# The seven products of a fast matrix multiplication in another order, in the two MLPs of a Trainium2 kernel

## The reference, cut to what matters

```python
for layer in range(2):
    h = rmsnorm(x, mix_norm_g[layer])
    if layer == 0:
        x = x + diff_attention(h, ...)
    else:
        x = x + recurrent_block(h, rec_w_x, rec_w_y, ...)    # h @ w_x and h @ w_y come first
    x = x + sqrelu_mlp(rmsnorm(x, mlp_norm_g[layer]), mlp_w1[layer], mlp_w2[layer])

def sqrelu_mlp(h, w1, w2):
    return jnp.square(jax.nn.relu(h @ w1)) @ w2
```

## Time and profile before

| | |
|---|---|
| median of 3 runs | 3581.73 us (3578.41 to 3583.86) |
| the profiled execution, its own time | 3583.34 us |
| its span, first to last instruction | 3581.2 us |
| PE busy (matmul) | 3399.5 us, 95% |
| DVE busy | 2466.7 us, 69% |
| ACT busy, POOL busy | 1558.7 us (44%), 757.0 us (21%) |
| first MLP, from the first product on PE | 651.3 to 1274.2 us |
| w_x to w_o of the recurrent layer | 1274.2 to about 1600 us |
| second MLP and its sums | about 1600 to 2246 us |

### The profile page before, as it was taken

One profiled execution on the slowest core, in us unless ns is written; L12 is line 12 of the kernel. 1 busy time (PEld: TensorE's weight loads), 2 busy tenths in 40 slices (PEclk: granted clock), 3 DMA queues, 4 the chain that ended last, 5 costly groups with the idle time before them and its releaser, 6 DMA issues. The chain is left out here.

```text
span 3581.2 us, 43257 instructions
## 1 busy us (share of the span) xinstructions
PE 3399.5 (95%) x17006; PEld 2668.2 (75%) x17006; DVE 2466.7 (69%) x2845; ACT 1558.7 (44%) x2241; POOL 757.0 (21%) x439
## 2 busy tenths in 40 slices
PE   7999999999999989999999998899989989998898
PEld 6777777878778778787878787887646778764567
DVE  4666765898888989649887989476546442374666
ACT  2355453545454436425454454116345320443551
POOL 2455551000000037420000000232211222230214
PEclk9999999999999999999999999899999999999999
DMA  4234341221111121211111210231042121202413
GB/s 168 90 127 150 112 165 70 70 67 47 48 48 47 59 89 47 96 64 47 47 48 60 68 62 1 88 124 51 21 135 60 65 106 47 74 33 65 126 69 112
DMA packets 100595, 275.27 MB, mean 77 GB/s; under 512 B 9872, under 2 KB 11824, under 8 KB 100400
## 3 DMA queue, kind: packets, MB, share of 16 engines
q1 hardware_dynamic: 77104, 206.52, 17.5%
q10 hardware_dynamic: 16384, 40.90, 3.5%
q0 software_dynamic: 6912, 25.17, 2.1%
HBM read 220.39 MB, written 47.97 MB: 75 GB/s over the span
## 5 line engine op out<-in xcount | busy, mean ns | idle before, releaser
L933 PE MATMUL tk_aux<-tk_t,tk_s_hi 128*128 128x512 f32 x2048 | 512.9, 391 | 13.8 <-ACT tk_aux L1061 7.3
L1038 ACT CAST tk_s_hi<-tk_w 128x1024 fp32r<-128x1024 f32 x224 | 235.5, 1052 | 521.0 <-PE tk_aux L933 292.5
L933 PEld LDWEIGHTS tk_aux<-tk_t,tk_s_hi 128*128 128x128 f32 x2048 | 381.3, 188 | 106.6 <-issue 19.4
L933 PE MATMUL tk_acc<-tk_t,tk_s_hi 128*128 128x512 f32 x1536 | 380.2, 390 | 0.0
L1259 DVE TENSOR_TENSOR held_lo<-tk_w,tk_s_hi 128x1024 fp32r<-128x1024 f32 x224 | 273.7, 1222 | 107.4 <-ACT tk_s_hi L1038 107.2
L933 PEld LDWEIGHTS tk_acc<-tk_t,tk_s_hi 128*128 128x128 f32 x1536 | 288.3, 188 | 60.7 <-issue 1.0
L933 PE MATMUL tk_aux<-tk_t,held_lo 128*128 128x512 f32 x1024 | 274.0, 389 | 0.0
L933 PEld LDWEIGHTS tk_aux<-tk_t,held_lo 128*128 128x128 f32 x1024 | 192.2, 188 | 40.5
L175 POOL TENSOR_TENSOR pj_w_lo<-pj_w_raw,pj_w_hi 128x1024 fp32r<-128x1024 f32 x24 | 61.8, 2578 | 702.0 <-ACT pj_w_hi L150 700.4
L933 PE MATMUL tk_acc<-tk_t,held_lo 128*128 128x512 f32 x768 | 205.3, 389 | 0.0
L841 POOL CAST held_hi<-held_raw 128x1024 fp32r<-128x1024 f32 (+1 forms) x30 | 41.5, 1384 | 710.2 <-DVE tk_t L1275 596.9
(11 more groups left out here) (474 smaller groups left out, 8196.2 us busy)
## 6 DMA issues: line engine op xcount, KB each, us to landing
tk_w<-in_w_trunk SPq DMA_DIRECT2D x128, 512.0 KB, 4.1
da_w_mod<-in_ada_w POOLq DMA_DIRECT2D x48, 512.0 KB, 4.0
pj_w_raw<-in_w_in SPq DMA_DIRECT2D x44, 512.0 KB, 3.3
held_raw<-in_w_trunk SPq DMA_DIRECT2D x26, 512.0 KB, 3.3
held_raw<-in_w_qkv SPq DMA_DIRECT2D x24, 512.0 KB, 4.2
ma_w_raw<-in_w_out SPq DMA_DIRECT2D x24, 512.0 KB, 3.3
x_dram<-xT ACTq DMA_DIRECT2D x16, 512.0 KB, 4.4
xT<-x_dram SPq DMA_DIRECT2D x16, 512.0 KB, 7.0
```

The source lines that it names most:

```text
L933: last = pe.matmul(bank, w[:, d % 2, at:at + P], tr[:, f % 2, y, k, :], start=(j in (M1, M4, M5) and k == 0 and part == 0), stop=(k == 3 a ...
L1038: act.copy(tiles(s_hi[:, d % 2, :]), left(d)).then_inc(sems["s_hi"], 1)
```

## The change

1. The order becomes M1, M2, M4, M5, M6, M7, M3. The loads, sums, takes, ReLUs and squares are re-timed to it: t3 is made two steps earlier (steps 8 and 9 instead of 10 and 11); at an even phase's end whole tiles 4 to 7 go through the ReLU first (step 13) and the half tiles 0 to 3 in the next phase's steps 0 and 1; t1, t2 and t4 of an odd phase follow in steps 1 to 3.
2. ACT takes M1 (and M4 to M6 of even phases) before the cast of the next right operand instead of behind it. In phases 0 and 8 the root, which belongs to that take, comes forward with it.
3. At both MLPs' ends the tiles come in the order 4, 5, 6, 7, 0, 1, 2, 3 (`TILES`), and part of the squares is added earlier.
4. The recurrent layer's sum (`total`) stands in the second w_x panel, ahead of its sixth tile. The third panel goes to `aux[:, 1]` and does not wait for a bank of `pn.acc`; DVE reads it there.

POOL's and SP's lists of instructions are the same, save for which block is loaded when and which unit is waited for.

```diff
-    M1, M2, M4, M5, M6, M3, M7 = range(7)
+    M1, M2, M4, M5, M6, M7, M3 = range(7)
...
                     def first_of_branch(k):
-                        if k == DK - 1:
+                        pe.wait_ge(sems["x_lo"], (k + 4) % DK + 1)
+
+                    def second_of_branch(k):
+                        if k == TILES[5]:
                             total(1, 0)
-                        pe.wait_ge(sems["x_lo"], k + 1)
...
                     pe.wait_ge(sems["read_dve"], wg.d_at[7, M7, 1])
-                    linear(R_X, first_of_branch, 1)
-                    pe.wait_ge(sems["read_dve"], wg.d_at[7, M7, 3])
-                    linear(R_X + 1, None, 3)
+                    pn.product(pe, 0, R_X // 2, *A, first_of_branch, TILES)
+                    pe.wait_ge(sems["read_dve"], wg.d_at[7, M3, 3])
+                    pn.product(pe, 1, R_X // 2, *A, second_of_branch, TILES)
+                    pn.product(pe, 0, R_X // 2 + 1, *A, bank=aux[:, 1, :], spare=True)
+                    linear(R_X + 3, None, 1)
+                    evacuated(pe, R_X + 2)
...
                                 if not (ph % 8 == 0 and d == 0 or ph % 8 == 7 and d == 13):
                                     s_high(at + 1)
-                                if ph % 2 and d < 2:
-                                    for p in (2 * d, 2 * d + 1):
-                                        square_tile(ph - 1, p)
-                                if f + 1 < 56 * m + 56:
-                                    t_high(f + 1, d % 2)
+                                if ph % 2 and d == 2:
+                                    for p in (2, 3):
+                                        square_block(ph - 1, 1, p)
...
                                     for p in (2 * q, 2 * q + 1):
                                         take(ph, jj, p)
+                                if f + 1 < 56 * m + 56:
+                                    t_high(f + 1, d % 2)
...
-                        for kind, n in (((low, 0), (low, 1)), ((low, 2), (low, 3)), ((low, 4), (low, 5)),
-                                        ((low, 6), (low, 7)) + tuple((partial(add_hidden_square, 1), n) for n in range(DK)))[step]:
+                        square = partial(add_hidden_square, 1)
+                        for kind, n in (((low, 4), (low, 5)), ((low, 6), (low, 7), (square, 4), (square, 5)),
+                                        ((low, 0), (low, 1), (square, 6)), ((low, 2), (low, 3), (square, 7), (square, 0),
+                                                                            (square, 1), (square, 2), (square, 3)))[step]:
```

More of the change, by code:

```diff
@@ L197, in credit, with product @@
             pe.sem_inc(self.sems[f"panel_done{u}"], 1)
-    def product(self, pe, u, turn, h_hi, h_lo, before_chunk=None, order=None, behind=None):
+    def product(self, pe, u, turn, h_hi, h_lo, before_chunk=None, order=None, behind=None, bank=None, spare=False):
         pe.wait_ge(self.sems[f"w_split{u}"], turn + 2)
-        pe.wait_ge(self.sems[f"psum_free{u}"], turn + 1)
+        if not spare:
+            pe.wait_ge(self.sems[f"psum_free{u}"], turn + 1)
         order = order or ([c.k for c in self.prep.chunks] if self.prep else list(range(self.kc)))
+        bank = self.acc[:, u, :] if bank is None else bank
         for k in order:
@@ L208, in product @@
                 for s in range(2):
-                    last = pe.matmul(self.acc[:, u, s * HALF:(s + 1) * HALF], w[:, u, k, :],
+                    last = pe.matmul(bank[:, s * HALF:(s + 1) * HALF], w[:, u, k, :],
                                      h[:, k, s * HALF:(s + 1) * HALF],
@@ L1194, in last @@
                     def last(step):
-                        for n in ((0, 1), (2, 3), range(4, DK))[step]:
+                        for n in ((4, 5), (6, 7), range(4))[step]:
                             final(1, n)
@@ L1386, in up @@
                                 take(*due[1])
+                            if d == 13:
+                                for p in (2, 3):
+                                    relu_tile(ph, p)
                     def down(ph, finish_step):
```

91 lines of the change are left out of this document (51 added, 40 removed).

## The result

The changed kernel takes **3596.98 us**, the median of 5 runs (3592.8 to 3602.85). The kernel before, measured beside it, has 3581.73. The ratio is 1.0043, with a 95% interval of 1.0031 to 1.0055: slower by about 15 us. The forecast was 3582.8 us in a range of 3573 to 3593, with "no change" as its likeliest case. The measured time lies outside that range: the forecast's sum was +1.05 us, and the difference is +15.2.

The account below looks back on a forecast made before the run. PE, busy 95% of the span, was taken to bound the kernel. Terms +1.15 + 0.4 + 1.0 - 1.5 = +1.05 us on the median of 3581.73 gave 3582.8 us, range 3573 to 3593.

Parts of the forecast that it names:

- no change: Whole kernel: time differs by less than a measurement can tell, about 0.2% or 7.2 us; chance 0.68.
- Part B: Eight borders from even to odd phase: loss stays, as one wait of about 2.1 us in M4; +0.4 us.
- Rival 3: Nine new waits, in M4 and panel 0, each followed by half clock: +15.3 us, 3598.1 us; 17%.
- The sign named for the forecast as a whole: Inside the MLPs: a PEclk below 1.0 in the profile after would make the whole forecast wrong.
- Rival 1: At the eight borders M4's operand comes in time and the loss goes: 21.2 us, 3561.2 us; 15%.
- Part A: Start of each MLP: DVE's reciprocals come later; +0.75 us for the second, +0.4 for the first, +1.15 us together.
- Part C: Handover to the recurrent layer: DVE and POOL collide, PE waits in panel 0, root comes later; +1.0 us.
- Part D: End of the second MLP: fewer takes behind the last split, so the last sums come earlier; -1.5 us.

Follow-up runs that it names:

- x1: Changed kernel with eight dummy matmuls on PE ahead of M4's first unit in each of the eight odd phases; 3587.66 us, ratio 1.0011.
- x2: Changed kernel with ACT's second-half squares all in step 1 and DVE's sums moved ahead of splits in odd phases; 3562.82 us, ratio 0.9944.
- x4: Changed kernel with ACT again casting M4's operand ahead of the root and M1's last two copies at each MLP's start; 3594.48 us, ratio 1.0036.
- x5: Changed kernel with DVE's squares at the handover to the recurrent layer behind all low parts; 3593.43 us, ratio 1.0038.
- x8: Changed kernel with four dummy matmuls on PE ahead of M4's first unit in each odd phase; 3585.34 us, ratio 1.0015.
- x9: Changed kernel with the edits of x2 and x4, plus PE waiting before M4 in odd phases until DVE took M2's fourth result; 3626.62 us.
- x11: Changed kernel with the edits of x2 and x4, plus PE waiting before M4 in odd phases until DVE took M2's second result; 3583.74 us.

## Why the prediction was wrong

**The step that failed is in Part B: it moved the border's loss into one wait of 2.1 us and put the granted clock behind that wait at nothing.** The term was +0.4 us; the runs show +1.0 us for the longer border and +9.8 us for seven stretches at half clock, and x1, with the waits filled, is 9.3 us faster. Rival 3 described what happened: the border's loss gathered into one wait in M4, the clock at 0.51 behind a wait of 2.02 us, 1.7 us for each stretch, 3598.1 us. The measurement is 3596.98, and that this is so near is partly luck: seven stretches of nine came, at 1.15 to 1.6 us each, where rival 3 counted nine and 15.3 us.

I gave rival 3 17% because the matmuls around the wait in the earlier trace rows seemed sparser than the MLP's, "six in 3.80 us". That was a misreading. Those matmuls are longer, not further apart, and 2.1 of their 3.80 us lie in the half-clock stretch itself. PE was busy for 3.45 of the 3.45 us behind the wait, and ahead of it without a gap too:

```profile
3307.86 6.53 PE L2359 MATMUL ma_sc<-ma_wv,xT 128*128 128x512 f32 x14 [0.26 <-ACT ma_more L2625]
```

So the row spoke for a fall between dense matmuls, and nothing in the trace of before showed that the MLP's PE is protected. The same trace had more to count: of its eight waits of PE of 2.0 to 3.2 us, seven had a stretch at half clock that began within 4.5 us of the wait's start. The sign named for the forecast as a whole, a PEclk below 1.0 inside the MLPs, is what came.

The rest of **Part B** was right in its mechanism and in the place: no wait in M2, one of 2.19 us in M4's first unit (forecast 2.1), DVE's low part 24.49 us after phase 3's start, at 910.61 (forecast 24.37, 909.75 less 885.38). Without the clock a border costs 0.13 us more, 1.0 us in all, where I took 0.4. But its reading "the same loss, in another place: nothing" was the error in small. A loss has a shape. Before, PE lost it as a wait of 0.65 us, one of 0.73 (for ACT's copy, inside M2) and slower matmuls; in one piece the same microseconds cost half as much again.

**Rival 1's price was right, and its argument was missed.** In the changed kernel the operand of M4 did not come in time, so rival 1 did not happen. But x2 takes all losses of the borders away and comes to 3562.8, where rival 1 said 3561.2. I had written that the chain before M4 "has PE's own M1 at its head". x2 shows that it hung on the order on DVE: a sum that needed no cast stood behind an instruction that did, and two waits of 1.17 us for casts, which I had counted as fixed parts of the chain, could be filled.

**Part A** is confirmed: 0.36 and 0.86 us in phases 0 and 8, forecast 0.4 and 0.75; x4 takes both back.

**Part C** is confirmed: the root comes 0.74 us later from panel 0's start (forecast 1.0), PE waits 2.41 and 1.10 us (2.9 and 1.5), the 9.5 us come back as 8.76 before panel 2, and the next MLP starts 0.9 us later. The forecast rested on DVE and POOL shutting each other out. The rows show it again: POOL's subtraction beside DVE's low parts took 3.56 us (2.42 alone), and the pair of low parts 4.22 (2.47 alone). The Trainium skill (SBUF — State Buffer, Who interferes with whom) gives the reason, an exclusive pair of ports; the trace agrees.

**Part D** failed, at -1.5 us. The last sums did not come earlier: from phase 15's first matmul to them it is 94.3 us before and 96.0 after, and less the stretch at half clock and the 0.13 us of the border some +0.1. DVE runs without a gap from 50.4 us (before) and 53.2 us (after) into phase 15 to the last sum, and its work in the phase is the same, 94 and 95 instructions, 89.4 and 89.7 us busy. I counted the takes saved behind the last split, but with DVE the limit an instruction moved from there to an earlier place in the same stretch saves nothing.

**The median** lies 15.2 us above the one before, 2 us more than the terms of the table give up to the last sums (13.0 without the start, which the change doesn't touch). In x1, x2, x5 and x8 a wait of 1.51 us in phase 8 is followed by a stretch at half clock, and in x1, x8, x9 and x11 the 2.4 us wait in panel 0 is; in the profiled run after neither is. That other runs of the changed kernel had such stretches would explain it, but they were not profiled. The stretch behind the sums, which no edit touches, also differs by up to 8 us from trace to trace, so 2 us need no cause in the change.

## What to carry to other kernels

Read a loss of the bounding engine by its shape as well as its sum: several waits under a microsecond and one of two microseconds are not the same where the engine's clock depends on being used. When an edit gathers waits into one, price a stretch of half clock behind each, by the nearest row, and let only a row speak against it. Check in the same row whether the engine was busy around the wait before calling it a different case. Then ask of the engine that is waited for which of its instructions stands behind one that waits itself: moving ready instructions into three such gaps was worth 34 us here between the changed kernel and x2, the clock's part included, while a few dummy matmuls in the wait were worth 9.

## What the runs showed of the hardware

How often a stretch at half clock followed an unbroken wait of PE between dense matmuls at the borders:

| Kernel | wait, us | followed by a stretch | its length, us |
|---|---|---|---|
| x1 | 0.39 | 0 of 8 | |
| x8 | 1.28 | 0 of 8 | |
| x11 | 1.80 | 4 of 8 | 3.41 |
| changed kernel | 2.19 | 7 of 8 | 3.41 |
| x4 | 2.19 | 6 of 8 | 3.41 |
| x5 | 2.19 | 7 of 8 | 3.41 |
| x9 | 6.41 | 8 of 8 | 6.83, once 10.24 |

A wait in phase 8, of 1.51 us, was followed by one in four kernels of five (the changed kernel's was not), and the wait of 2.4 us in panel 0 in four of nine. So the same wait sometimes costs 1.15 to 1.6 us on top and sometimes nothing, and a longer wait at another place was not always the likelier one to cost. What decides it in a single case no run here shows. In such a stretch ten matmuls pass in 3.41 us, and sixteen at full clock. The Trainium skill (TensorE: Matmul & The Clock Gate, What's actually happening) has the same two levels, 1.2 and 2.4 GHz; the granted clock of 0.50 and 1.00 in these windows agrees.
